# One 512-column product for the high and the low tokens in the first feed-forward's up units

## The reference

```python
D_MODEL, SEQ, D_FF, FFN_CONV = 1024, 256, 2816, 3
...
h = rms_norm(x, pre_ffn_norm[l])
u = causal_dwconv(h @ ffn_w_up[l], ffn_conv_w[l], ffn_conv_b[l])
gate, val = jnp.split(u, 2, axis=-1)
f = (jax.nn.gelu(gate, approximate=True) * val) @ ffn_w_down[l]
x = x + rms_norm(f, post_ffn_norm[l])
```

## Time and profile before

| | us |
|---|---|
| median of 3 runs | 879.27 |
| the three runs | 879.27, 873.22, 879.78 |
| time of the profiled execution | 876.9 |
| its span in the trace | 875.1 |
| PE busy in it | 854.2 (98%) |
| DVE busy | 594.1 (68%) |
| ACT busy | 461.2 (53%) |
| mean granted clock of PE | 0.994 |

### The profile page before, as it was taken

One profiled execution on the slowest core, in us unless ns is written; L12 is line 12 of the kernel. 1 busy time (PEld: TensorE's weight loads), 2 busy tenths in 40 slices (PEclk: granted clock), 3 DMA queues, 4 the chain that ended last, 5 costly groups with the idle time before them and its releaser, 6 DMA issues.

```text
span 875.1 us, 15552 instructions
## 1 busy us (share of the span) xinstructions
PE 854.2 (98%) x6234; PEld 794.5 (91%) x6234; DVE 594.1 (68%) x780; ACT 461.2 (53%) x650; POOL 63.3 (7%) x64
## 2 busy tenths in 40 slices
PE   6999999999999999999999999999999999999997
PEld 6999999999988998899999998898887889999995
DVE  4548986537867587697767777876564686656554
ACT  5457772448656344575545556565464553333332
POOL 0025920000000321000000000000000000000000
PEclk9999999999999999999999999999989999999999
DMA  9644452333442456464564556254423365555531
GB/s 344 227 145 145 146 197 94 117 124 135 145 145 97 169 193 212 150 231 172 178 207 163 192 192 204 91 187 146 145 79 138 121 232 201 191 181 180 182 130 48
DMA packets 22167, 143.82 MB, mean 164 GB/s; under 512 B 2928, under 2 KB 3188, under 8 KB 5728
## 3 DMA queue, kind: packets, MB, share of 16 engines
q1 hardware_dynamic: 20304, 138.30, 44.8%
q0 software_dynamic: 1808, 4.73, 1.6%
HBM read 141.96 MB, written 1.84 MB: 164 GB/s over the span
## 4 chain that ended last, share of the span: by engine, by line
PE 91%; ACT 3%; DVE 3%; issue 1%; DMA 1%; SPq 0%; DVEq 0%; ACTq 0%
PE pj L467 18%; PE pj L469 15%; PE pj L470 15%; PE pa L891 7%; PE pa L892 7%; PE pa L893 7%; PE pj L471 2%; PE pj L472 2%; PE pa L506 2%; PE pj L570 1%; ACT w_hi L1154 1%; PE pj L576 1%; PE pj L572 1%; DVE area L1640 1%; PE po L605 1%
## 5 line engine op out<-in xcount | busy, mean ns | idle before, releaser
L1627 DVE TENSOR_TENSOR w_lo<-w_raw,w_hi 128x2048 fp32r<-128x2048 f32 x127 | 294.4, 2320 | 71.0 <-ACT w_hi L1154 70.8
L467 PE MATMUL pj<-a_hi,w_hi 128*128 128x256 f32 x1168 | 333.1, 285 | 0.7 <-issue 0.7
L470 PE MATMUL pj<-a_hi,w_lo 128*128 128x256 f32 x1168 | 330.4, 283 | 0.0
L469 PE MATMUL pj<-a_lo,w_hi 128*128 128x256 f32 x1168 | 330.4, 283 | 0.0
L1154 ACT ACTIVATE w_hi<-w_raw 128x2048 fp32r<-128x2048 f32 x127 | 242.0, 1907 | 56.7 <-PE pa L893 42.4
L467 PEld LDWEIGHTS pj<-a_hi,w_hi 128*128 128x128 f32 x1168 | 223.9, 192 | 4.9 <-issue 3.9
L469 PEld LDWEIGHTS pj<-a_lo,w_hi 128*128 128x128 f32 x1168 | 223.9, 192 | 0.9
L470 PEld LDWEIGHTS pj<-a_hi,w_lo 128*128 128x128 f32 x1168 | 223.9, 192 | 0.0
L891 PE MATMUL pa<-w_hi,a_hi 128*128 128x512 f32 x280 | 109.3, 390 | 1.4 <-issue 1.4
L892 PE MATMUL pa<-w_lo,a_hi 128*128 128x512 f32 x280 | 109.2, 390 | 0.0
L893 PE MATMUL pa<-w_hi,a_lo 128*128 128x512 f32 x280 | 108.9, 389 | 0.0
(11 more groups left out here) (272 smaller groups left out, 1028.8 us busy)
## 6 DMA issues: line engine op xcount, KB each, us to landing
w_raw<-stream SPq DMA_DIRECT2D x127, 1024.0 KB, 4.8
area<-gains POOLq DMA_DIRECT2D x4, 512.0 KB, 4.2
cst<-consts SPq DMA_DIRECT2D x1, 1093.0 KB, 13.6
x_tok<-x_in SPq DMA_DIRECT2D x2, 512.0 KB, 4.8
w_raw<-stream SPq DMA_DIRECT2D x4, 256.0 KB, 7.0
area<-cmpw POOLq DMA_DIRECT2D x1, 1024.0 KB, 5.7
out<-x_tok SPq DMA_DIRECT2D x4, 256.0 KB, 2.0
t_wide<-t_rows POOLq DMA_DIRECT2D x1, 768.0 KB, 11.3
```

The costliest lines, as they stand in the source:

```text
L467: pe.matmul(out_, a[0], a[1], start=first, stop=False)
L469: pe.matmul(out_, wh, al, start=False, stop=False)
L470: return pe.matmul(out_, wl, ah, start=False, stop=last)
L1627: dve.tensor_tensor(w_lo[:, slot, :], w_raw[:, slot, :], w_hi[:, slot, :].bitcast(F32), ALU.subtract)\
```

## The change

The high and low tokens now lie side by side in one tensor, `a_hl[:, k, 0:2, :]`, so one 512-column matmul multiplies the high weights with both. Its result fills a whole bank: high-by-high in columns 0 to 255, high-by-low in 256 to 511. A second matmul of 256 columns adds low weights by high tokens to the first half. A chunk (gate and value) takes two banks, so the two pairs are `pjo[0:2]` for odd and `pjo[2:4]` for even chunks; `po` is now the fourth bank of `pjo`. The loop over k is outside and the halves `nb` inside, so the two banks alternate. This holds for chunks 2 to 21; chunks 0 and 1 stay as they were.

Behind such a unit, ACT copies the two low halves out of PSUM into a new buffer `us` (`up1_low`), DVE adds the two other halves (`up1_sum`), and, one product later, multiplies `us` by the norm into `fxs[e]` (`up1_scale`). On ACT the gelu of an even chunk moves behind the copy of the next one, that of the odd chunk to the end of the step.

```diff
-            def up1(u, slot, b, n):
-                unit_ready(u)
-                bank_free(b, n)
-                unit_b(slot, b)
+            def two_bank_unit(slot, s):
+                for k in range(KC):
+                    both = a_hl[:, k, :, :].rearrange("p a t -> p (a t)")
+                    for nb in range(2):
+                        c = k * 256 + nb * P
+                        bank = two_banks[s][:, nb, :]
+                        pe.matmul(bank[:, 0:2 * T], w_hi[:, slot, c:c + P], both, start=(k == 0), stop=False,
+                                  skip_group_check=True)
+                        mm = pe.matmul(bank[:, 0:T], w_lo[:, slot, c:c + P], a_hi[:, k, :], start=False,
+                                       stop=(k == KC - 1), skip_group_check=True)
+                mm.then_inc(S("unit_done"), 1)
...
-            for c in (2, 3):
-                up1(u0 + c, (u0 + c) % SLOTS, c % 3, FFN1_BANK0[c % 3] + c // 3)
+            await_read(pe, "O", "rbc1")
+            bank_free(2, FFN1_BANK0[2])
+            unit_ready(u0 + 2)
+            two_bank_unit((u0 + 2) % SLOTS, 0)
+            bank_free(0, FFN1_BANK0[0] + 1)
+            bank_free(1, FFN1_BANK0[1] + 1)
+            unit_ready(u0 + 3)
+            two_bank_unit((u0 + 3) % SLOTS, 1)
...
                 for e in range(2):
-                    b = (2 * q + e) % 3
-                    up1(u + e, (u0 + 1 + e) % 3, b, m * 2 + (FFN1_BANK0[b] + (2 * q + e) // 3))
+                    unit_ready(u + e)
+                    pe.wait_ge(S(f"up1_read{e}"), i - 1)
+                    two_bank_unit((u0 + 1 + e) % 3, e)
...
+            def up1_low(c, e):
+                act.activation(us, two_banks[e][:, :, T:2 * T], ACT.Copy).then_inc(S("up1_low"), 1)
...
+            def up1_sum(c, e):
+                dve.wait_ge(S("up1_low"), c - 1)
+                tt(us, two_banks[e][:, :, 0:T], us, ALU.add).then_inc(S(f"up1_read{e}"), 1)
+
+            def up1_scale(i, e):
+                dve.wait_ge(S(f"up1_read{e}"), i)
+                tt(fxs[e], us, rbc2, ALU.mult).then_inc(S("fx_ready"), 1)
```

More of the change, by code:

```diff
@@ L57 @@
 FFN1_BANK0 = list(_uses)
-for _c in range(UP1):
-    _uses[_c % 3] += 1
+for _c in range(2):
+    _uses[_c] += 1
 for _n, _name in enumerate(n for n in UNITS2 if n[0] != "wo2"):
@@ L163, in program @@
         t5_wide = nc.dram_tensor("t5_wide", (4, P, 384), F32, kind="Internal").ap()
-        pj3 = pb("pj", [P, 3, 512])
-        pj = [pj3[:, i, :] for i in range(3)]
+        pjo = pb("pjo", [P, 4, 512])
+        pj3, po = pjo[:, 0:3, :], pjo[:, 3, :]
+        pj = [pjo[:, i, :] for i in range(3)]
         pa = pb("pa", [P, 4, 512])
         ps, pt = pa[:, 0:2, :], pa[:, 2:4, :]
-        po = pb("po", [P, 512])
         def V(kib, *dims):
@@ L333, in fo @@
             return pj[f3_first][:, 0:T] if j % 2 else po[:, 0:T]
+        two_banks = (pjo[:, 2:4, :], pjo[:, 0:2, :])
+        us = V(12, 2, T)
         block = ctx.enter_context(nc.Block())
@@ L1448, in _, with up1_tap2 @@
             fw, fb = PCOLS["fw"][0], PCOLS["fb"][0]
-            def up1_tap2(c, b, n, e):
-                act.wait_ge(S(f"pj_read{b}"), n + 1)
+            def up1_low(c, e):
+                act.activation(us, two_banks[e][:, :, T:2 * T], ACT.Copy).then_inc(S("up1_low"), 1)
+            def up1_tap2(c, e):
+                if isinstance(c, int) and c < 2:
+                    act.wait_ge(S(f"pj_read{c}"), FFN1_BANK0[c] + 1)
+                else:
+                    act.wait_ge(S("fx_ready"), c - 1)
                 for m in range(2):
@@ L1468, in _ @@
             ahead(u0 + 1)
[L1469 to L1470 removed]
+            up1_tap2(0, 0)
+            up1_tap2(1, 1)
             ahead(u0 + 2)
@@ L1476, in _ @@
             for c in (2, 3):
-                up1_tap2(c, c % 3, FFN1_BANK0[c % 3] + c // 3, c % 2)
+                act.wait_ge(S("unit_done"), u0 + c + 1)
+                up1_low(c, c % 2)
+                if c == 3:
+                    up1_gelu(2, 0)
+                up1_tap2(c, c % 2)
                 up1_hi(c - 1, 8 + c - 1, (c - 1) % 2)
@@ L1480, in _ @@
                     ahead(u0 + 4)
-                up1_gelu(c, c % 2)
+            up1_gelu(3, 1)
             def ffn1_step(i, m, q, last=False):
                 for e in range(2):
-                    b, c = (2 * q + e) % 3, i * 2 + e
-                    up1_tap2(c, b, m * 2 + (FFN1_BANK0[b] + (2 * q + e) // 3), e)
+                    c = i * 2 + e
+                    act.wait_ge(S("unit_done"), i * 3 + (u0 - 1 + e))
+                    up1_low(c, e)
+                    if e:
+                        up1_gelu(c - 1, 0)
+                    up1_tap2(c, e)
                     up1_hi(c - 1, 8 + (2 * q + e - 1) % 6, 1 - e)
                     split(u0 + 1 + 3 * q + e, m * 3)
-                    up1_gelu(c, e)
+                up1_gelu(c, 1)
                 if last:
@@ L2095, in up1_out, with up1_taps @@
                 tt(fxs[e], two(pj[b]), rbc2, ALU.mult).then_inc(S(f"pj_read{b}"), 1)
-            def up1_taps(c, b, n, e):
-                dve.wait_ge(S(f"pj_read{b}"), n + 1)
+            def up1_sum(c, e):
[4 more added lines that the diff above has]
+                tt(fxs[e], us, rbc2, ALU.mult).then_inc(S("fx_ready"), 1)
+            def up1_taps(c, e):
+                if isinstance(c, int) and c < 2:
+                    dve.wait_ge(S(f"pj_read{c}"), FFN1_BANK0[c] + 1)
+                else:
+                    dve.wait_ge(S("fx_ready"), c - 1)
                 dve.wait_ge(S("tap2"), c * 2 + 2)
```

24 lines of the change are left out of this document (13 added, 11 removed).

## The result

The changed kernel takes 879.09 us (median of 20 runs), the one before 876.02 beside it (20 runs): ratio 1.0038, 95% interval 1.0021 to 1.0054, so slower by 1.8 to 4.7 us. The three runs shown ahead of the prediction had their median 3 us above that of twenty. Forecast were 0.9 us of gain and 877.5 us; the time lies in the range, the direction is wrong.

The account below looks back on a forecast made before the run. PE was taken to bound the kernel, with DVE full at the feed-forward's start. Terms -4.3 (matmuls) + 0.3 (fourth bank) + 3.1 (wait) = -0.9 us gave 876.0 or, from the median, 878.4; forecast 877.5 between them, range 871.5 to 882.

Parts of the forecast that it names:

- the walk through the two orders: Feed-forward's start: DVE's and ACT's fixed orders followed chunk by chunk; unit 7's low split starts 4.15 us later.
- the wait for unit 7: Behind the first down unit, PE waits 3.1 us for DVE's low weight split of the next up unit.
- the fourth bank: Feed-forward's start: unit 2 must wait until the norm is copied out of that bank, 0.3 us lost.
- no wait in the loop: Feed-forward loop: the added ACT and DVE work is covered, with 0.4 to 0.6 us of slack per step.
- The rival of the late loop: Feed-forward loop: DVE's chain exceeds its slack, PE waits in each of 9 steps; 0.5 us over gives 880.5; chance 0.10.
- That of alternating banks: Changed up units: changing banks every second matmul lowers the clock in each of 9 steps, 902 us; chance 0.02.
- What PE saves: Matmuls of 20 changed chunks: 13.5 ns saved per pair, 320 pairs, 4.3 us in all.
- Two signs that I had set myself: Changed profile: loop steps of 16.5 to 16.6 us would confirm; wide and narrow distances not adding to 0.35 would refute.
- Merging gains nothing: Changed up units stay at 5.76 us, PE's wait shrinks to 2.25, giving 879.4 us; chance 0.04.
- "Rivals", the clock: Behind PE's 3.1 us wait, one half-clock stretch costs 2.9 us more, giving 878.9 us; chance 0.10.

Follow-up runs that it names:

- grouped kernel: Changed kernel with, per k, both 512-column products first, then both 256-column ones; 881.23 us, ratio 1.0036 to the kernel before.
- exchanged loops: Changed kernel with the loop over halves outside and k inside, so a bank gets its sixteen products in a row; 877.41 us, ratio 1.0026 to before.
- the kernel with both products wide: Changed kernel with the second product also 512 columns wide, adding the low-by-low term; one run, 912.40 us.
- not merged: Changed kernel with each 512-column product split back into two 256-column ones, all else kept; 880.12 us, ratio 1.0047 to before.
- the two loop kernels: Kernel before with DVE's low split repeated in each of six hardware-loop steps, the second with 512 columns more; one run each, 904.97 and 902.99 us.
- late split: Kernel before with DVE's low split of unit 7 done three times over, so TensorE waits; 881.24 us, ratio 1.0070 to before.
- changed, again: Changed kernel measured a second time, nothing altered; 879.58 us, ratio 1.0046 to before.
- storage alone: Kernel before with only the changed kernel's joined token tensor and joined PSUM banks, products and orders as before; 876.56 us, ratio 0.9980 to before.
- early splits: Changed kernel with unit 7's weight split moved earlier on ACT and DVE, those of units 8 and 9 moved up one place; 875.36 us, ratio 0.9969 to before.
- early and grouped: Changed kernel with the weight splits moved earlier and, per k, both wide products ahead of both narrow ones; 872.03 us, ratio 0.9959 to before.
- filled wait: Changed kernel with eleven idle-product calls behind the first down unit, to keep TensorE working through the wait for unit 7; 882.55 us, ratio 1.0077 to before.
- before, filler: Kernel before with six idle-product calls behind the first down unit, holding TensorE up without standstill; 879.47 us, ratio 1.0051 to before.

## Why the prediction was wrong

**Right.** The stretch that decides, the start with DVE at 16.10 of 17 us, was found in the profile of before, and the walk through the two orders gave each station within 0.15 us: the wait for unit 7 on DVE's split (3.1 forecast, 2.90 and 2.48 measured), the fourth bank (0.3), no wait in the loop. Unit 7 begins 31.30 us behind the start of the norm's copy; the prediction has 405.7 - 374.41 = 31.29. The rival of the late loop is out: even the grouped kernel with its shorter step has none. That of alternating banks is out by the exchanged loops and by the kernel with both products wide, whose banks alternate at an even 0.2267 us a product.

**Wrong, step "What PE saves".** It priced a pair at the sum of two paces, 0.2265 + 0.12, and took the transitions in the earlier trace rows for proof. A single transition, read to 0.01 us, can't carry a term of 0.0135 times 320. A pair in the loop is 0.3528: 7 ns are saved, not 13.5. Over 20 units, 2.2 us or a little more (at the start one trace had 0.348) instead of 4.3, and the down unit behind takes 0.04 more, which the prediction put at nothing. The sum by my own steps, with the mean of the two waits, is then -2.2 + 0.4 + 0.3 + 2.7 = +1.2, close to FF's 0.9 to 1.1. That turns the sign. It is plainer from unit 7 on, because its date is set by DVE whatever PE saved ahead of it. Up to there the changed kernel loses 31.30 - 28.76 = 2.54 us, as forecast; behind it lie 16 units, which should have given back 3.4 us and gave 1.4 (177.35 - 31.30 = 146.05 against 176.24 - 28.76 = 147.48). The whole error of FF is in these 2.0 us. Two signs that I had set myself point at it: steps of 16.5 to 16.6 us, which came out at 16.79, and distances that don't add to 0.35, which was too coarse to show 0.353. With the grouped order the pace of the prediction is nearly reached, and the step comes to 16.59 against its 16.55. The rival *Merging gains nothing* had 879.4, next to the 879.09 measured, but that is a coincidence: against the not merged kernel the merging is worth 1.5 us of FF. That the time lies in the forecast range is no merit of the sum either, since the range spans 10.5 us.

**Wrong, "Rivals", the clock.** I put it at 0.10 and argued that the slow stretch of the earlier trace rows wasn't tied to a stop. A stop in mid-feed-forward was in no row, and it can lower the clock: 7 of 12 waits in the two loop kernels, and the one of the late split, came with half clock from about their end on, 1.3 to 2.9 us lost each. In the two traces of the changed kernel, and in those of its three variants with a wait of 2.1 to 2.8, the clock behind the wait stayed at 1.00, so its share in their medians, about 1 us, is an estimate from the loop kernels and not shown at this place.

**The account.** 1.1 in FF and about 1.0 of clock would make 2.1; measured are 1.8 to 4.7. The record has more than the medians: the span and the mean granted clock of every execution. Span times clock is what the span would be at full clock throughout; the rest is what counts as lost to half clock. (A part of that rest, 0.3 to 1.9 us in the traces, lies at the very end, when TensorE is done.) Below, each kernel's mean is given as a difference to before, in us, with two standard errors. Before is that beside it; for the first row it is all 84 runs of before that have both numbers.

| kernel (runs) | FF, one trace | span x clock | lost to half clock |
|---|---|---|---|
| changed (20) | +1.1 | +1.6 ± 0.4 | +1.5 ± 1.4 |
| changed, again (12) | +0.9 | +1.1 ± 0.6 | +3.3 ± 2.2 |
| storage alone (12) | 0.0 | -0.1 ± 0.7 | -0.8 ± 2.1 |
| early splits (12) | -1.6 | -1.1 ± 0.6 | -0.8 ± 1.1 |
| grouped widths (10) | -0.5 | -0.3 ± 0.6 | +3.5 ± 2.2 |
| not merged (10) | +2.6 | +3.4 ± 0.6 | +0.9 ± 2.5 |
| halves outside (10) | +0.9 | +1.7 ± 0.6 | +0.1 ± 2.6 |
| early and grouped (12) | -3.6 | -3.7 ± 0.5 | -0.8 ± 1.5 |
| filled wait (8) | +2.9 | +2.9 ± 0.7 | +3.1 ± 1.6 |
| before, late split (7) | +4.8, of it 1.7 clock | +2.5 ± 1.0 | +3.7 ± 2.4 |
| before, filler (12) | +2.6 | +2.5 ± 0.9 | +1.8 ± 2.3 |

At full clock the kernels differ from before by what their FF says, within 0.8 us. The remainder of the medians is low clock. Taken together, before loses 4.8 ± 0.7 us to it (84 runs), the three kernels without a hold-up at unit 7 lose 4.3 ± 0.7 (36 runs), the ones where TensorE stood still there 6.9 ± 0.8 (69 runs), and the two where it worked through a filler 6.7 ± 1.3 (20 runs). So being held up in the feed-forward goes with some 2 us more of low clock. That the standstill itself brings them is not shown: the filled kernels lose as much, and in the traces of the changed kernel no low stretch lies behind the wait; they lie ahead of the feed-forward and in the second block. Coming later doesn't explain it either, since the grouped kernel is no later than before and loses the most. The cause stays open.

**What the wait cost in all.** Early splits against the changed kernel: the ratios to before, 0.9969 and 1.0038, differ by 0.7%, some 6 us, of which FF explains 2.7; the recorded clocks put most of the rest on low clock (+1.5 and +3.3 us in the changed kernel's two series, -0.8 with early splits). The change as such, products and added work, is a gain once one split stands elsewhere.

## What to carry to other kernels

Before adding a pass to an engine, look for the stretch where it is already full, not at its mean, and walk its order there; the first late item may be a job for a later stage, which can simply be moved up. Take the price of an instruction mix from a long run of that mix, not from single transitions, when the term is a few nanoseconds times hundreds. A hold-up of TensorE of 2 to 5 us in the middle of a full stretch cost more than its length here on average, in low clock, whether it stood still or was given filler. And where the granted clock of every run is recorded, span times clock separates a kernel's own change from such losses.

## What the runs showed of the hardware

- 512-column products run 0.2265 us apart among themselves and 256-column ones 0.120, but in turn they take 0.353 a pair, 6 ns over the sum; in twos (wide, wide, narrow, narrow) 0.348. The bank doesn't matter. At the start of the feed-forward the same alternation took 0.348 in one trace and 0.355 in four.
- Waits of 2.55 to 2.8 us brought TensorE's clock to 1.2 GHz at 3 of 6, waits of 3.3 to 3.5 us at 4 of 6, one of 3.0 us at 1 of 1; each time TensorE had been busy at 2.4 GHz until the wait. Five waits of 2.1 to 2.9 us at unit 7 left it at 2.4 GHz.
- The runs of one and the same kernel (before, 84 of them) have spans from 870.5 to 878.7 us and mean granted clocks from 1.000 to 0.989; span times clock stays at 870, with a standard deviation of 1.0 us where the span has 2.6.
